# PEER gates by cell scatters instead of one-hot matmuls, and a third buffer for activations and gates

## The reference, cut to what matters

```python
q = einsum('td,dhq->thq', x1, w_query)                    # 8 heads, two halves each
scores = einsum('thpc,hpnc->thpn', q, sub_keys)            # 128 keys for each half
s_top, i_top = top_k(scores, 16)
cand = s_top[:, :, 0, :, None] + s_top[:, :, 1, None, :]   # 256 candidates a head
best, pos = top_k(cand, 16)
expert_idx = i*128 + j of the 16 best                      # 128 experts a token
gates = softmax(best)
act = gelu(einsum('td,tkd->tk', x1, expert_u[expert_idx]))
ffn = einsum('tk,tkd->td', act * gates, expert_v[expert_idx])
out = layer_norm(alpha * x1 + ffn)
```

## Time and profile before

| | us |
|---|---|
| median of 3 runs (2007.53, 2012.72, 2030.52) | 2012.72 |
| the profiled execution: its time | 2017.35 |
| its span, first to last instruction | 2015.6 |
| PE busy | 1963.3 (97%) |
| DVE, POOL, ACT busy | 1106.5, 889.4, 680.6 |

### The profile page before, as it was taken

How to read it: one execution, slowest core, us unless ns; L and a number is a source line. 1 busy time by engine, 2 the same in 40 slices (tenths; PEclk the granted TensorE clock), 3 DMA queues, 4 the chain that set the end, 5 groups by cost and what they waited for, 6 DMA issues and landing times.

```text
span 2015.6 us, 24624 instructions
## 1 busy us (share of the span) xinstructions
PE 1963.3 (97%) x9433; PEld 1563.4 (78%) x9433; DVE 1106.5 (55%) x2263; ACT 680.6 (34%) x1029; POOL 889.4 (44%) x502
## 2 busy tenths in 40 slices
PE   7999999999989999999999999999998999999998
PEld 5766655888778888888888888888886778878876
DVE  4022212311330599883688888500076879888887
ACT  4623323323222333233333333332332333333332
POOL 6313111344344144545333333344487857576540
PEclk9999999999999999999999999999999999999999
DMA  5202110232422144444465566654488989999993
GB/s 192 75 31 74 53 48 21 73 110 95 167 84 94 61 148 142 141 150 147 161 196 178 182 194 198 209 198 147 141 318 301 374 332 384 337 351 381 352 354 115
DMA packets 164774, 368.39 MB, mean 183 GB/s; under 512 B 15265, under 2 KB 80929, under 8 KB 164530
## 3 DMA queue, kind: packets, MB, share of 16 engines
q1 hardware_dynamic: 51264, 184.57, 26.1%
q10 hardware_dynamic: 90866, 115.06, 16.8%
q0 software_dynamic: 22528, 67.19, 8.9%
HBM read 305.96 MB, written 60.82 MB: 182 GB/s over the span
## 4 chain that ended last, share of the span: by engine, by line
PE 74%; DMA 11%; DVE 8%; issue 3%; POOL 3%; ACT 1%; SPq 0%; ACTq 0%; DVEq 0%; POOLq 0%
PE bank L432 22%; PE bank L434 21%; PE bank L433 21%; DMA act<-activation_scratch 11%; PE bank L715 3%; DVE w_lo L1334 2%; DVE bank L1199 2%; POOL weight L395 2%; PE bank L564 1%; DVE act L1323 1%; DVE wt_lo L1327 1%; PE bank L586 1%; PE bank L603 1%; PE bank L611 1%; PE bank L682 1%
## 5 line engine op out<-in xcount | busy, mean ns | idle before, releaser
L383 POOL TENSOR_TENSOR w_lo<-stage,w_hi 128x1024 fp32r<-128x1024 f32 x224 | 543.1, 2433 | 910.3 <-ACT w_hi L773 910.3
L432 PE MATMUL bank<-x_hi,w_lo 128*128 128x512 f32 x1376 | 543.6, 395 | 7.6 <-DVE x_lo L1056 5.0
L434 PE MATMUL bank<-x_hi,w_hi 128*128 128x512 f32 x1376 | 537.4, 391 | 0.0
L433 PE MATMUL bank<-x_lo,w_hi 128*128 128x512 f32 x1376 | 536.9, 390 | 0.0
L773 ACT ACTIVATE w_hi<-stage 128x1024 fp32r<-128x1024 f32 x348 | 358.9, 1041 | 21.9 <-PE bank L434 8.9
L432 PE MATMUL bank<-w_hi,wt_lo 128*128 128x512 f32 x768 | 301.7, 393 | 21.0 <-DVE wt_lo L1327 21.0
L432 PEld LDWEIGHTS bank<-x_hi,w_lo 128*128 128x128 f32 x1376 | 259.1, 188 | 62.5 <-DVE x_lo L1056 5.9
L434 PEld LDWEIGHTS bank<-x_hi,w_hi 128*128 128x128 f32 x1376 | 259.1, 188 | 55.3
L434 PE MATMUL bank<-w_hi,wt_hi 128*128 128x512 f32 x768 | 300.4, 391 | 0.0
L433 PE MATMUL bank<-w_lo,wt_hi 128*128 128x512 f32 x768 | 300.4, 391 | 0.0
L433 PEld LDWEIGHTS bank<-x_lo,w_hi 128*128 128x128 f32 x1376 | 259.4, 189 | 52.4
(11 more groups left out here) (217 smaller groups left out, 1902.4 us busy)
## 6 DMA issues: line engine op xcount, KB each, us to landing
stage<-in_expert_uT SPq DMA_DIRECT2D x128, 512.0 KB, 3.5
stage<-in_expert_v SPq DMA_DIRECT2D x128, 512.0 KB, 7.2
stage<-in_mix_stream SPq DMA_DIRECT2D x84, 512.0 KB, 3.5
gates<-gate_scratch ACTq DMA_DIRECT2D x32, 768.0 KB, 6.2
act<-activation_scratch ACTq DMA_DIRECT2D x32, 768.0 KB, 12.7
activation_scratch<-act_out_a ACTq DMA_DIRECT2D x64, 256.0 KB, 2.3
activation_scratch<-act_out_b ACTq DMA_DIRECT2D x64, 256.0 KB, 2.3
gate_scratch<-gstage_a ACTq DMA_DIRECT2D x6, 2048.0 KB, 11.1
```

Source lines behind the costliest of these rows:

```text
L383: nc.gpsimd.tensor_tensor(w_lo[:, slot, 0:width], stage[:, slot % STAGE, 0:width], w_hi[:, slot, 0:width], ALU.subtract).then_inc(split_do ...
L432: mm(dst, l_lo, r_hi, start=first, stop=False)
L433: mm(dst, l_hi, r_lo, start=False, stop=False)
L434: return mm(dst, l_hi, r_hi, start=False, stop=last)
```

## The change

First, the gates. `gate_dram` is laid out as [tile i, j, token] and filled with zeros by 32 transfers on SP's queue, one behind each load of the tiles 10 to 41. When a dense block's top 16 is done, DVE computes for each pick the cell's number (`cells`), and POOL adds the gate to that cell by an indirect DMA: one DMA for one pick of all 128 tokens of a block, 3 x 128 = 384 of them (`scatter_head`). The two picks of a token in different heads may fall on one cell, so the 16 DMAs of a head wait until the head before them in the same block has landed; two blocks alternate. The one-hots, the matmuls, the turns, their copies and stores go. The sparse block is now the last, the dense ones the first three. POOL splits only the first 14 tiles of U; DVE splits all the others, between the steps of its top 16, where a clock counted at build time says that a split is due (`passed`).

Second, three units of activations and gates are held. Unit u+2 is loaded when unit u-1 is used up. The first units' activations are loaded at tile 120, the gates at tile 126, when all scatters have landed. The last norm's gain and bias go to another place and are loaded two tiles later.

```diff
@@ constants
-GB = 32 ... FIRST_GATE = 50; GATE_SPAN = 48
+FILLS = 32; FIRST_FILL = 10; UNITS_HELD = 3
+TILE_US = 5.44; POOL_TILES = 14; FIRST_BEST_US = -13.0
+EXP_AT = {7: 0, 21: 1, 36: 2, 51: 3}
 def on_vector(tile):
-    return tile >= NKEY + 4
+    return tile >= POOL_TILES
@@ SP
+            def zero_fill(f):
+                ...
+                u = NKEY * ND // P // FILLS
+                cells = gate_dram.rearrange("i j t -> (i j t)").rearrange("(p n c) -> p n c", p=P, c=P)
+                sp.dma_start(cells[:, u * f:u * f + u, :],
+                             zeros[:].unsqueeze(1).broadcast_to([P, u, P])).then_inc(zero_filled, 16)
+                if FIRST_FILL <= n < FIRST_FILL + FILLS:
+                    zero_fill(n - FIRST_FILL)
@@ POOL
-            for tile in range(NKEY + 4):
+            for tile in range(POOL_TILES):
                 split_low(first_expert + tile, (first_expert + tile) % RING, QW)
+            def scatter_head(b, h):
+                if h == 0:
+                    pool.wait_ge(scat_ready, 2 * b + 2)
+                else:
+                    pool.wait_ge(scattered[b], 16 * HEAD_PICKS * h)
+                for k in range(h * HEAD_PICKS, (h + 1) * HEAD_PICKS):
+                    nc.gpsimd.indirect_dma_start(out=gate_cells,
+                                                 out_offset=bass.IndirectOffsetOnAxis(ap=scat_idx[:, b, k:k + 1], axis=0),
+                                                 in_=scat_gate[:, b, k:k + 1], in_offset=None,
+                                                 compute_op=ALU.add).then_inc(scattered[b], 16)
+            pool.wait_ge(zero_filled, 16 * FILLS)
+            for h in range(4):
+                scatter_head(0, h)
+            for b in range(DENSE):
+                for h in range(4):
+                    scatter_head(b, h + 4)
+                    if b + 1 < DENSE:
+                        scatter_head(b + 1, h)
@@ PE
             for tile in range(NKEY):
-                if tile in TURN_AT:
-                    turn_picks(TURN_AT[tile])
                 score_tile(tile)
-                for g in range(groups_by(tile - 1), groups_by(tile)):
-                    gate_group(g)
-            pe.wait_ge(gm_evac, NGROUP)
-            pe.wait_ge(parts_ready, TB - 1)
@@ ACT, score stage
                 store_tile(t)
-                for g in range(groups_by(t - 1), groups_by(t)):
-                    evac_group(g)
-                if t == last_group_tile + 2: ... load_unit(0); load_unit(1)
+                if t == NKEY - 8:
+                    load_acts(0)
+                    load_acts(1)
                 if t == NKEY - 2:
-                    round_weight(0)
+                    load_gates(0)
+                    load_gates(1)
+            load_acts(2)
+            load_gates(2)
+            round_weight(0)
@@ ACT, value stage
-                if v % UNIT == 0 and v // UNIT + 1 < NUNIT:
+                if v % UNIT == 0 and v // UNIT + 2 < NUNIT:
                     sc.wait_ge(wt_done, v)
-                    load_unit(v // UNIT + 1)
+                    load_acts(v // UNIT + 2)
+                    load_gates(v // UNIT + 2)
@@ DVE
+            def passed(us):
+                clock[0] += us
+                while next_split[0] <= clock[0] / TILE_US + 3:
+                    split_value(next_split[0])
+                    next_split[0] += 1
+                    clock[0] += 1.25
             def top16(vals, idx, src, rows_n):
+                us = 0.2 * rows_n if rows_n == HP else 0.34 * rows_n
                 for a in range(rows_n):
                     ins = v.max(vals[:, a, 0:8], src[:, a, :])
                 step(ins)
+                passed(us)
                 ...
+                passed(1.6 * us)
```

More of the change, by code:

```diff
@@ L1275, in _ @@
-            first_level(0)
-            second_level(0)
-            decode(0)
-            step(v.scalar_tensor_tensor(out=spare[:], in0=ijg[:, 0, 0, :], scalar=float(NKEY), in1=ijg[:, 0, 1, :],
-                                        op0=ALU.mult, op1=ALU.add))
-            v.tensor_copy(eidx[:], spare[:])
-            step(v.tensor_scalar(spare[:], spare[:], float(S), None, ALU.mult))
-            step(v.tensor_scalar(spare[:], spare[:], token[:], None, ALU.add))
-            v.tensor_copy(aidx[:], spare[:]).then_inc(eidx_ready, 1)
@@ L1284, in _, with cells @@
-            for t in range(1, TB):
+                dst = g0 if t == DENSE else scat_gate[:, t, :]
+                ins = v.tensor_tensor(dst.rearrange("p (h k) -> p h k", h=PH), gx, share, ALU.mult)
+                if t < DENSE:
+                    ins.then_inc(scat_ready, 1)
+                else:
+                    step(ins)
+            def cells(dst, t, width):
+                step(v.tensor_scalar(spare[:], spare[:], float(width), float(t * P), ALU.mult, ALU.add))
+                step(v.tensor_scalar(spare[:], spare[:], token[:], None, ALU.add))
+                return v.tensor_copy(dst, spare[:])
@@ L1285, in _, with expert_numbers @@
+            def expert_numbers(t):
+                step(v.scalar_tensor_tensor(out=spare[:], in0=ijg[:, t % 2, 0, :], scalar=float(NKEY), in1=ijg[:, t % 2, 1, :],
+                                            op0=ALU.mult, op1=ALU.add))
+            for t in range(TB):
                 first_level(t)
-                finish_gates(t - 1)
                 second_level(t)
-                if t >= 2:
-                    split_gates(t - 1)
                 decode(t)
-            finish_gates(TB - 1)
@@ L1312, in _ @@
-            for g in range(NGROUP):
-                if g == 8:
-                    split_gates(TB - 1)
-                one_hots(g)
+                expert_numbers(t)
+                if t < DENSE:
+                    cells(scat_idx[:, t, :], t, ND).then_inc(scat_ready, 1)
+                else:
+                    v.tensor_copy(eidx[:], spare[:])
+                    cells(aidx[:], t, S).then_inc(eidx_ready, 1)
+                finish_gates(t)
+                passed(3.0)
+            for tile in range(next_split[0], NKEY):
+                split_value(tile)
```

186 lines of the change are left out of this document (63 added, 123 removed).

## The result

The changed kernel takes 2082.64 us (median of 4 runs, 2064.32 to 2086.83) where the kernel before took 2019.51 (4 runs, the three of the table above and one of 2026.3). The ratio is 1.0274, with an interval of 1.0225 to 1.0323. It is slower, and outside the range of the prediction.

A forecast was written before the change was run, and what follows sets the result against it. PE's own work was taken as the bound, busy 1963.3 of 2015.6 us. Gate matmuls -72.9 and third unit -11.4, other terms 0, took the median 2012.7 to 1928.4, rounded to 1929; range 1916 to 1968.

The forecast's parts named there:

- Scatters: POOL's 384 scatters beside the score stage: 1.35 us each, last landed at 1314 (bounds 1237 and 1404), before 1380; cost 0.
- the scatter that adds is a longer instruction: Rival on POOL's queue: at double the 0.94 us, period 2.29, scatters end 295 us late, time 2224, slower; chance 0.11.
- its sign: Trace sign on POOL for the longer-instruction rival: a mean scatter over 1.25 us, where the forecast expected near 1.05.
- The forecast's threshold for the period: POOL's scatters: an average period up to 1.5 us is hidden by the score stage; each 0.1 above costs 38 us.
- Collisions of POOL and DVE: Score stage: a gather meeting a DVE split's start takes 1.76 us for 0.94, 0.83 more per hit; half the collisions taken.
- Gate matmuls -72.9: Score stage, PE's queue: removing the gate matmuls takes it from 769.2 to 696.3 us, tiles 5.44 us apart.
- splits on DVE 0: Score stage: moving splits from POOL to DVE, a load of 22%, costs 0; bounds 0 and +20 us.
- zero fills 0: SP's queue: 32 fills of 768 KB, some 4.2 us each, cost 0; bounds 0 and +3 us.
- The seam without late scatters: Between score and value stages: first value tile at 1388, PE ready at 1384.0, +4; net 0, bounds -1 and +6.
- Third unit -11.4: Value stage: loads issued seven tiles ahead instead of three remove 11.4 us of PE waits; bounds -11.4 and +6.
- the DMA-bound rival: Value stage: DMA is the bound, so the third unit brings nothing or -6, time 1940 to 1946; chance 0.12.
- the picks' shorter waits: Start of the value stage: PE, 4 us later, finds the sparse block's two pick waits of 8.1 us 4 us shorter.

The follow-up runs named there:

- the writing kernel: Changed kernel with the 384 scatters writing the gate instead of adding it, sums of double picks left out: 1924.87 us, ratio 0.9586; run again elsewhere 2387.94 and 1924.61 us.
- the third unit alone: Kernel before with only a third unit of activations and gates held, gates still from one-hot matmuls: 2003.13 us against 2008.68, ratio 0.997.
- the two kernels with sums: Changed kernel with DVE summing double picks and scatters writing: unpaced 2196.95 us; with at most four scatters per finished score tile 2079.82 us.

## Why the prediction was wrong, point by point

- **Scatters: the step that failed.** "The nearest row is the gather of one float a partition. Alone it takes 0.94 us." The adding scatter takes 1.547. Its period without the landings is 1.93 ((622.3 + 118.1) / 384) where the term had 1.35. Both bounds were made from the gather, so they bounded collisions and landings, not the instruction, and a wait of 131 us lay outside them. What came was the rival "the scatter that adds is a longer instruction", which had a chance of 0.11, and its sign too: the mean is 1.62 us, over the 1.25 named. Its working was near: 1.547 + 0.30 + 0.11 = 1.96 against 1.93. The forecast's threshold for the period, 1.5, kept 50 us apart for decodes and landings. The measured 1.98 has these in it, and against it all of the 634 us count, 1.65 a scatter: (1.98 - 1.65) x 384 = 127, measured 131. The landings themselves were short, 19.5 us for nine.
- **Collisions of POOL and DVE: right, and the rule wrong here.** A scatter that starts within a split takes longer, here 0.95 us:

```profile
1101.30 1.55 POOL L420 DMA_INDIRECT gate_scratch<-scat_gate,scat_idx  x1 [0.30 <-issue]
1103.15 2.50 POOL L420 DMA_INDIRECT gate_scratch<-scat_gate,scat_idx  x1 [0.30 <-issue]
```
```profile
1103.01 1.23 DVE L1198 TENSOR_TENSOR w_lo<-stage,w_hi 128x1024 fp32r<-128x1024 f32 x1 [4.15 <-ACT w_hi L771]
```

  The Trainium skill (SBUF — State Buffer, "Who interferes with whom") infers that a `tensor_tensor` does not hold up descriptor generation. As in the earlier trace rows the trace disagrees. By the means (against the medians) it is 0.15 us a write and 0.07 us an adding scatter. With writes the last ended at 1307.5; the forecast was 1314.
- **Gate matmuls -72.9, splits on DVE 0, zero fills 0: right.** Score tiles 5.44 us apart, 0.3 us lost in 696. The mixing stage kept PE busy for 397.52 us of 400, as in the earlier trace rows. A fill landed in 6.4 us by the median where I estimated 4.2, and it cost nothing.
- **The seam without late scatters: right.** 3.4 us of wait in the writing kernel, forecast 4.
- **Third unit -11.4: the mechanism right, the size half of it by the medians (5.5 us).** The waits past 1541 went, as forecast. From 1650 to 1700 us of the changed kernel PE is never idle at a DMA share of 1.01 and 375 GB/s, so the DMA-bound rival is refuted.
- **A stretch in which PE stalls without a wait: in no case of mine.** It cost the changed kernel some 30 us (the estimate above). What the value stage had lost before went at the same time, so the table shows only +6.7.

With a scatter as short as the forecast took it, the writing kernel took 1924.87 where 1929 was said. Part of that is luck. Between the profiles of the third unit alone and of the writing kernel, both on chip 0, the score stage gives -72.8 and the seam +3.6 (forecast -72.9 and +4). The value stage gives -6.8, where the forecast had 4 for the picks' shorter waits, and 3.3 us come from ahead of the score stage. Those 6.1 us were in no term, and they stand in for the 5.9 by which the third unit fell short.

## What to carry to other kernels

Price an indirect DMA that adds by itself: it is another instruction for POOL than a gather or a write (1.55 against 0.95 us), and here 384 in a row on one queue turned 0.6 us each into a wait of 131 us. When both bounds of an unknown cost are made from one row of another kind, the rival that says "the kind is different" deserves more than 0.11. Measure an experiment and its control on the same chip before reading a cause from their difference.

## What the runs showed that was not expected

- An adding scatter of one float a partition: POOL 1.547 us, 144 packets of its queue for a DMA; a write: 0.958 us, 32 packets.
- On two of four chips, while POOL issued indirect DMAs every 1.25 us, PE's matmuls stood 1.4 us and more apart (5 of them in the 25 us of the slowest line shown). In the score stage DVE and ACT nearly stopped then, and the DMA share fell to 0.02; on the other two the same kernel and the same rate of POOL left PE at 222 matmuls in 50 us. In the two kernels with sums on chip 3 each long stretch ended as POOL paused or was through. That a held-up DVE makes no splits, and so leaves POOL undisturbed at its fastest, fits the runs as what feeds it, but was not tested by itself; what starts it, and what differs between the chips, stays open.
